# The last output tile next to a layer norm, multiplied one token half after the other

## The reference

```
h = swiglu(modulate(x, 0), w_ffn1_in, w_ffn1_out)
x = layer_norm(ALPHA*x + 0.5*gate0*h, gain0, bias0)        # layer norm 0
mix = concat(pool_out, nsa_out) @ w_out                    # attention, pooling: unchanged here
x = layer_norm(ALPHA*x + gate1*mix, gain1, bias1)          # layer norm 1
h = swiglu(modulate(x, 2), w_ffn2_in, w_ffn2_out)
x = layer_norm(ALPHA*x + 0.5*gate2*h, gain2, bias2)

layer_norm: mu = mean(x); var = mean((x-mu)^2); (x-mu)*rsqrt(var+1e-5)*gain + bias
modulate(x, s) = x*(1 + scale_s) + shift_s                 # scale, shift, gate come from w_ada and c
```

## Time and profile before

| what | value |
|---|---|
| runs | 1324.28, 1324.5, 1325.3 us; median 1324.5 |
| profiled execution | 1326.14 us, of which the span from first to last instruction 1324.5 us |
| mean granted clock of TensorE | 0.987 |
| PE busy | 1277.7 us, 96% |
| DVE, ACT, POOL busy | 569.8, 439.9, 189.8 us |

### The profile page before, as it was taken

How to read it: one execution, slowest core, us unless ns; L and a number is a source line. 1 busy time by engine, 2 the same in 40 slices (tenths; PEclk the granted TensorE clock), 3 DMA queues, 4 the chain that set the end, 5 groups by cost and what they waited for, 6 DMA issues and landing times.

```text
span 1324.5 us, 25199 instructions
## 1 busy us (share of the span) xinstructions
PE 1277.7 (96%) x9736; PEld 1150.8 (87%) x9736; DVE 569.8 (43%) x969; ACT 439.9 (33%) x681; POOL 189.8 (14%) x372
## 2 busy tenths in 40 slices
PE   6999999999999999998998998999999999999997
PEld 3899999999999999996656667989999999988875
DVE  2532222222333356215567766683233332332466
ACT  3322222222211135226456654253222222223343
POOL 3000000000000026552380060142000000030000
PEclk9999999999999998999989999989999999999999
DMA  9545454454352236863740075512322223364463
GB/s 299 165 125 157 128 176 142 133 181 130 106 166 86 75 106 149 186 141 97 227 123 2 4 205 145 174 34 81 94 80 79 79 79 95 95 195 130 140 201 129
DMA packets 217370, 170.16 MB, mean 128 GB/s; under 512 B 47048, under 2 KB 198904, under 8 KB 217225
## 3 DMA queue, kind: packets, MB, share of 16 engines
q1 hardware_dynamic: 210657, 151.37, 39.4%
q0 software_dynamic: 6640, 17.82, 4.7%
HBM read 164.75 MB, written 8.63 MB: 131 GB/s over the span
## 4 chain that ended last, share of the span: by engine, by line
PE 89%; DVE 5%; ACT 3%; issue 1%; DVEq 1%; DMA 1%; SPq 0%; ACTq 0%
PE ps L340 60%; PE ps L939 10%; PE ps L299 3%; PE ps L2486 2%; PE ps L1172 1%; ACT AR L1882 1%; PE ps L1670 1%; PE ps L282 1%; PE ps L1687 1%; DVE AR L2519 1%; PE ps L1223 1%; DVE AR L2047 1%; PE ps L2685 1%; PE ps L1779 1%; PE ps L1246 1%
## 5 line engine op out<-in xcount | busy, mean ns | idle before, releaser
L340 PE MATMUL ps<-UH,WH 128*128 128x288 f32 x1648 | 354.8, 296 | 1.0 <-DVE WL L259 1.0
L340 PE MATMUL ps<-UL,WH 128*128 128x288 f32 x1648 | 350.9, 294 | 0.0
L340 PE MATMUL ps<-UH,WL 128*128 128x288 f32 x1648 | 350.2, 293 | 0.0
L259 DVE TENSOR_TENSOR WL<-RAW,WH 128x1024 fp32r<-128x1024 f32 x134 | 165.3, 1234 | 324.5 <-ACT WH L255 321.0
L340 PEld LDWEIGHTS ps<-UH,WH 128*128 128x128 f32 x1648 | 262.8, 188 | 7.4 <-issue 6.2
L340 PEld LDWEIGHTS ps<-UL,WH 128*128 128x128 f32 x1648 | 264.8, 187 | 0.0
L340 PEld LDWEIGHTS ps<-UH,WL 128*128 128x128 f32 x1648 | 263.6, 187 | 0.0
L255 ACT ACTIVATE WH<-RAW 128x1024 fp32r<-128x1024 f32 x134 | 140.9, 1052 | 140.6 <-PE ps L340 134.8
L939 PE MATMUL ps<-WH,H 128*128 128x512 f32 x380 | 97.3, 398 | 0.0
L705 DVE TENSOR_TENSOR T<-MU,ps 128x576 f32<-128x576 f32 x44 | 33.2, 754 | 145.7 <-PE ps L340 143.6
L533 POOL TENSOR_TENSOR AR<-AR 128x576 f32<-128x576 f32 x12 | 19.8, 1648 | 516.9 <-ACT AR L450 455.9
(11 more groups left out here) (377 smaller groups left out, 1503.5 us busy)
## 6 DMA issues: line engine op xcount, KB each, us to landing
RAW<-in_w_ffn_in_dram SPq DMA_DIRECT2D x88, 512.0 KB, 3.9
AW<-in_w_ada_dram SPq DMA_DIRECT2D x42, 512.0 KB, 4.5
RAW<-in_w_ffn_out_dram SPq DMA_DIRECT2D x36, 512.0 KB, 3.5
AR<-in_w_ada_dram SPq DMA_DIRECT2D x7, 1024.0 KB, 11.2
RAW<-in_w_ffn_out_dram SPq DMA_DIRECT2D x16, 448.0 KB, 3.9
AR<-in_w_ada_dram SPq DMA_DIRECT2D x14, 512.0 KB, 5.9
RAW<-in_w_in_dram SPq DMA_DIRECT2D x28, 256.0 KB, 4.0
AW<-in_w_ffn_out_dram SPq DMA_DIRECT2D x14, 512.0 KB, 3.5
```

The costliest lines, as they stand in the source:

```text
L259: nc.vector.tensor_tensor(WL[:, slot, :], RAW[:, slot, :], WH[:, slot, :].bitcast(F32), ALU.subtract).then_inc(split_done, 1)
L340: mm = nc.tensor.matmul(ps[:, 2 * uslot + h, 0:HT], W[:, wslot, k * P:(k + 1) * P], R[:, k0 + k, h * HT:(h + 1) * HT], start=(first and k ...
```

## The change

Tile 7 is computed token half by token half. `product_halves` takes the place of `product` for the chunk that finishes tile 7: the loop over h is outermost, half 0 signals `half_mm`, and a function `between` is called between the halves. For layer norm 0 that is the third chunk alone (7 pieces, `between` does nothing); for layer norm 1 it is the whole product, and `between` is the summing of `RS`. The residual, the deviation, the square and the sums of the tile are made per half.

```diff
+        def product_halves(pe, n, wslot, k0, nk, RH, RL, first, between):
+            pe.wait_ge(split_done, n + 3)
+            for h in range(2):
+                for k in range(nk):
+                    for q, (W, R) in enumerate(((WH, RH), (WH, RL), (WL, RH))):
+                        mm = nc.tensor.matmul(ps[:, 2 + h, 0:HT], W[:, wslot, k * P:(k + 1) * P],
+                                              R[:, k0 + k, h * HT:(h + 1) * HT],
+                                              start=(first and k == 0 and q == 0), stop=(k == nk - 1 and q == 2))
+                if h == 0:
+                    mm.then_inc(half_mm, 1)
+                    between()
+            mm.then_inc(chunk_mm, 1)
...
         def ln_pe(pe, i):
             pe.wait_ge(sq_summed, i + 1)
             token_sums(SQS[i][:, 0, :], 4, NT).then_inc(stat_mm, 1)
+            pe.wait_ge(half_ready, i + 1)
+            token_sums(XT[:, KT - 1, :], 5, 0, 0, NT // 2)
+            pe.wait_ge(slot_free[0], SL0[f"ln{i}"][0] + 1)
+            pe.wait_ge(sq_ready, SQN * i + KT)
+            token_sums(SQS[i][:, KT - 1, :], 0, 0, 0, NT // 2)
             pe.wait_ge(stat_in, Z_LAST(i))
-            token_sums(XT[:, KT - 1, :], 5, 0).then_inc(stat_mm, 1)
-            pe.wait_ge(slot_free[0], SL0[f"ln{i}"][0] + 1)
-            pe.wait_ge(sq_ready, KT * (i + 1))
-            token_sums(SQS[i][:, KT - 1, :], 0, 0).then_inc(stat_mm, 1)
+            token_sums(XT[:, KT - 1, :], 5, 0, NT // 2, NT).then_inc(stat_mm, 1)
+            pe.wait_ge(sq_ready, SQN * i + KT + 1)
+            token_sums(SQS[i][:, KT - 1, :], 0, 0, NT // 2, NT).then_inc(stat_mm, 1)
...
+        def square_halves(act, i):
+            for h in range(2):
+                sq = SQS[i][:, KT - 1, h * HT:(h + 1) * HT]
+                act.wait_ge(dev_ready, SQN * i + KT + h)
+                nc.scalar.activation(sq, sq, ACT.Square).then_inc(sq_ready, 1)
...
         def residual_last(dve, i, gate, count):
+            dve.wait_ge(half_mm, i + 1)
+            nc.vector.scalar_tensor_tensor(out=z[:, 0:HT], in0=ps[:, 2, 0:HT], scalar=g[:, 0:1], in1=z[:, 0:HT],
+                                           op0=ALU.mult, op1=ALU.add).then_inc(half_ready, 1)
+            nc.vector.drain()
+            deviation_half(i, 0)
             dve.wait_ge(chunk_mm, count)
...
-            nc.vector.scalar_tensor_tensor(out=z[:, 0:HT], in0=ps[:, 2, 0:HT], scalar=g[:, 0:1], in1=z[:, 0:HT],
-                                           op0=ALU.mult, op1=ALU.add)
...
-            deviations(dve, i, KT - 1, KT)
+            deviation_half(i, 1)
...
         def ln_act(act, i, mod):
             hi(act, *split_args(AFTER[mod], 1))
-            squares(act, i, KT - 1, KT)
+            square_halves(act, i)
...
+                    if j == 5:
+                        product_halves(pe, CH0[b] + it * 6 + j, (CH0[b] + j) % 2, k0, nk, HH, HL, False, lambda: None)
+                        continue
...
-                hook = {4: pivot_sums, 7: part_sums}.get(j)
+                hook = pivot_sums if j == 4 else None
+                if j == KT - 1:
+                    product_halves(pe, CH0[a] + j, (CH0[a] + j) % 2, 0, KT, UH, UL, True, lambda: part_sums(pe, 1))
+                    continue
```

More of the change, by code:

```diff
@@ L205, in build @@
         PIVOT_MM, PIVOT_BC, PART_MM, ZLAST_MM, SQLAST_MM, MEAN_BC, RSTD_BC = (lambda i, q=q: 7 * i + q + 1 for q in range(7))
+        half_mm, half_ready = sem("half_mm"), sem("half_ready")
         dev_ready = sem("dev_ready")
@@ L398, in build, with token_sums @@
         BMU, BRS = ps[:, 6:8, 0:HT], ps[:, 4:6, 0:HT]
-        def token_sums(src, bank, col):
-            for j in range(NT):
+        def token_sums(src, bank, col, j0=0, j1=NT):
+            for j in range(j0, j1):
                 mm = nc.tensor.matmul(ps[0:TT, bank, col + j:col + j + 1], src[:, j * TT:(j + 1) * TT], ONE[:, 0:1],
@@ L445, in deviations, with deviation_half @@
                 nc.vector.tensor_tensor(tok2(SQS[i][:, m, :]), tok2(XT[:, m, :]), BMU, ALU.subtract).then_inc(dev_ready, 1)
+        SQN = KT + 1
+        def deviation_half(i, h):
+            c = slice(h * HT, (h + 1) * HT)
+            nc.vector.tensor_tensor(SQS[i][:, KT - 1, c], XT[:, KT - 1, c], BMU[:, h], ALU.subtract).then_inc(dev_ready, 1)
+        def square_halves(act, i):
[3 more added lines that the diff above has]
+                nc.scalar.activation(sq, sq, ACT.Square).then_inc(sq_ready, 1)
         def squares(act, i, m0, m1):
             for m in range(m0, m1):
-                act.wait_ge(dev_ready, KT * i + m + 1)
+                act.wait_ge(dev_ready, SQN * i + m + 1)
                 nc.scalar.activation(SQS[i][:, m, :], SQS[i][:, m, :], ACT.Square).then_inc(sq_ready, 1)
         def residual_last(dve, i, gate, count):
+            g, z, buf = ADA[:, GATE[gate] + KT - 1, :], XT[:, KT - 1, :], T2[:, 0, 0:TS]
+            dve.wait_ge(half_mm, i + 1)
[3 more added lines that the diff above has]
+            deviation_half(i, 0)
             dve.wait_ge(chunk_mm, count)
-            g, z, buf = ADA[:, GATE[gate] + KT - 1, :], XT[:, KT - 1, :], T2[:, 0, 0:TS]
             nc.vector.tensor_tensor(buf.rearrange("p (b t) -> p b t", b=NB),
@@ L530, in ln_pool @@
             for m in range(1, KT - 1):
-                pool.wait_ge(sq_ready, KT * i + m + 1)
+                pool.wait_ge(sq_ready, SQN * i + m + 1)
                 pool.drain()
```

## The result

The changed kernel takes 1327.42 us (median of 12 runs, 1326.35 to 1328.59), the kernel before 1325.21 us (12 runs, 1324.05 to 1327.01). The ratio is 1.0015, 95% interval [1.0008, 1.0022]. So it is slower, by 2.2 us, where 0.7 us less was forecast, and its time lies outside the predicted range (1321.8 to 1326.8). 0.7 us of the distance from the forecast 1323.8 is the kernel before itself: the prediction started from the median of three runs, 1324.5, and twelve give 1325.21. A second set of 11 runs on another chip gave 1.0014 [1.0005, 1.0023].

What follows compares the result with a forecast made beforehand. PE was taken as the bound, busy 96% of the span and 89% of the chain. Layer norm 0 -1.2, layer norm 1 +0.5, order 0 gave -0.7 us: from median 1324.5 to 1323.8, range 1321.8 to 1326.8.

Steps and rivals of the forecast that it cites:

- Layer norm 0, DVE, ACT and PE's sums: Layer norm 0: half 0's work under the product brings the first scaling 1.5 to 1.6 us earlier.
- What arrives: Layer norm 0: 1.2 us of the earlier scaling is saved in the whole kernel, bounds 0 and 3.2.
- The wait for the sums of RS: Last w_out product: PE stands still 1.3 us for DVE's last addition to RS; product ends 1.2 us later.
- the clock behind the stop: Half 1 of the last w_out product: no fall counted, 24 matmuls and the sums' 0.94 us priced at full rate.
- rival A: Clock falls inside the last w_out half: 1.7 us there, 1.7 more later, total +2.7, 1327.2, slower; chance 0.13.
- The 0.73 us saved in layer norm 1: Layer norm 1: DVE's list behind the product 0.73 us shorter; with the product's end 1.2 later, 0.5 us lost.
- Rival B: Layer norm 0: PE's row of waits eats the halves' gain, margin 0.25; +0.2, 1324.7, no change; chance 0.15.
- Order inside the product: Tile 7's product: one bank in a row and alternating weights cost 0, end of the range 1.9 us.
- Rival D: Tile 7's product: one bank in a row slows it by 1.9; total +1.2, 1325.7, no change; chance 0.07.
- Rival C: Layer norm 0's 1.2 GHz stretch one third shorter, 1.7 us more, layer norm 1 0.5: -2.9, 1321.6, faster; chance 0.10.

Runs made afterwards that it cites:

- e2: Kernel before with only layer norm 1 in halves, sums of RS after 24 matmuls as in the changed kernel: 1328.65 us, ratio 1.0030.
- e3: Changed kernel with the sums of RS late, in half 1 ahead of piece 4, after 36 of 48 matmuls: 1324.24 us, ratio 0.9993 to the kernel before.
- e4: Changed kernel with nine extra 288-column matmuls, results unused, filling PE's stop ahead of the sums of RS: 1324.37 us, ratio 0.9995 to the kernel before.
- e7: e3 with half 1's residual sums put ahead of half 0's squares' sums: 1323.20 us, ratio 0.9986 to the kernel before.
- e10: Kernel before with only layer norm 1 in halves, late sums of RS and residual sums first as in e7: 1326.08 us, ratio 1.0003.
- e5: Kernel before, no halves, with the sums of RS ahead of piece 4 instead of 6 in tile 7's product: 1329.03 us, ratio 1.0025.
- e1: Kernel before with only layer norm 0 in halves, w_out and layer norm 1 as before: 1324.66 us, ratio 1.0000.
- e9: Layer norm 0 alone in halves against the kernel before, a repeat of e1: 1323.96 us, ratio 0.9995.
- e12: The changed kernel timed again against the kernel before: 1327.54 us, ratio 1.0014.
- e6: e5 with nine extra 288-column matmuls, results unused, filling PE's stop ahead of the sums of RS: 1327.54 us, ratio 1.0020 to the kernel before.

## Why the prediction was wrong, point by point

- **Layer norm 0, DVE, ACT and PE's sums: right.** Forecast 1.5 to 1.6 us to the first scaling, found 1.7; variance forecast at 495.15, found 495.21; squares 0.90 for two. What arrives was put at 1.2 us; the runs of layer norm 0 alone neither confirm nor exclude it.
- **The wait for the sums of RS: the mechanism right, its size too small.** Stop forecast 1.3, found 1.24. But the product's end was put 1.2 us later, and the ruler says 1.5 with the clock held (8.91 - 7.39). Of the 0.3 us, 0.12 are a slip of the sum: it took the old end from the chain, where 12 matmuls count 1.70 us, and the new end from 24 x 0.132, while 12 x 0.132 is only 1.58. The rest is in small pieces. From where the next matmul would have started to the first sum it is 1.41 us (861.82 - 860.28 - 0.13) and not 1.3, and from the first sum to the next matmul 1.04 us (861.82 to 862.86) and not 0.94.
- **The failed step: the clock behind the stop was put at nothing, and rival A was given 0.13.** The fall is what happened, in every profile with the open stop. The forecast's path had the clock at 1.00 through half 1, counted its 24 matmuls at 3.17 us, and priced layer norm 1 at 0.5 us lost. The chain has them at 4.84 us, the clock costs 1.5 us in the product, and e2 says 3.3 us for layer norm 1. The argument against A was a stretch with six short matmuls in 2 us that kept its clock. It was weighed as if it told of this case; the rows of the layer norms themselves told more. There the clock had fallen 2.8 us and 2.0 us after the last wide matmul, with PE at the same kind of sums that now stand in the product for 2.1 of 2.9 us and 1.8 of 2.0 us. 1.24 us idle plus 1.04 of such sums is the same kind of stretch. Of A's price, the 1.7 us in the product were about right (1.5). Its other 1.7, a later low stretch over wider work, no run shows: that stretch began 2.0 us behind the product's end and lasted 10.2 us, both as before. That A's total of +2.7 came near the measured +2.2 is in part luck, since the 0.3 us of delay and the 0.5 us of lost shortening below stand in for it.
- **The 0.73 us saved in layer norm 1: they need the clock or the right order of the sums.** First scaling after the product's end: before 7.67, changed 7.49, e3 7.82; e4, where the clock fell only 4.3 us after that end, 6.98; with the residual's sums first 6.94 (e7) and 7.06 (e10). Rival B's mechanism (PE's row of sums eats the gain) was placed in layer norm 0, with a margin of 0.25 us; it decided in layer norm 1, where DVE's mean waited 0.63 us:

```profile
871.16 0.16 DVE L509 SCALAR_TENSOR_TENSOR STT<-ps,STT 96x6 f32<-96x6 f32 x1 [0.63 <-PE ps L417]
```

- **Order inside the product: right, cost 0.** With a stop of equal length the halves (e2, 10.41) and the pairs (e5, 10.42) take the same time, and without one 7.41 and 7.39. Rival D is out. The changed kernel has 9736 weight loads for 9736 matmuls, like the kernel before. By the Trainium skill's rule on sharing a weight load (TensorE: Matmul & The Clock Gate, "Step-by-step: what each phase is for") the new order would have needed more loads than the old one; the trace doesn't agree.
- **Rival C: the shorter stretch came, but not from the halves.** The low stretch of layer norm 0 was 6.8 us in this profile instead of 10.1. With the same layer norm 0 it was 10.2 in e3 and e4, 6.8 in e1 and e9, and 3.4 in e12. In e5, whose layer norm 0 is that of the kernel before, it was 6.8 too. It varies between executions and can't be counted on.

The sum as it should have been: -1.2 (layer norm 0) + 1.5 (delay) + 1.5 (clock) - 0.2 (shortening left) = +1.6, against +2.2 [1.1, 2.9] measured. The first term no run shows by itself.

## What to carry to other kernels

When an order changes, check each thing that sits inside the moved stretch against the time when its input is ready, not only the thing that was to be moved: a wait that "waits for nothing" had 36 matmuls of cover, and 24 were too few. Price a stop of PE as the stop plus what its clock does afterwards. Before splitting work into halves, put the small sums in the order in which their readers need them.

## What the runs showed of the hardware

- One stop of 1.24 us (e5: 1.26) followed by 1.04 us of one-column matmuls took the clock from 2.4 to 1.2 GHz for about 3.4 us in all four profiles that have it (e12: 860.5 to 863.8), and nine matmuls of 288 columns in the stop prevented it in both (e4, e6). The fall came 2.5 us (changed kernel) to 3.7 us (e5) after PE ran dry. A matmul of 288 columns then came every 0.24 us instead of 0.132.
- In layer norm 0 the stretch at 1.2 GHz had different lengths with the same instructions: 6.8 us in e5 (494.8 to 501.6) and 10.2 in e10 (494.3 to 504.5), both with the layer norm 0 of the kernel before; 6.8 in the changed kernel's first profile and 3.4 in e12. Runs of one kernel differ in their mean clock as well, and the time goes with it: e4's fell into a group at 0.988 (7 runs, 1323.97 to 1326.28) and one at 0.992 (4 runs, 1322.59 to 1323.50). That the low stretches in the layer norms make this difference is not shown, since only profiled runs have windows.
